# Depthwise convolution: ScalarE opens VectorE's two tap chains in PSUM, three ring slots in place of four, and sums left apart in four chunks

## The reference

```python
def conformer_conv(h, w1, b1, w_dw, b_dw, ln_g, ln_b, w2, b2):
    u = jnp.einsum('bsd,de->bse', h, w1) + b1
    a, gate = jnp.split(u, 2, axis=-1)
    u = a * jax.nn.sigmoid(gate)
    u = lax.conv_general_dilated(
        u, w_dw[:, None, :].astype(u.dtype),
        window_strides=(1,), padding=[(CONV_WIDTH - 1, 0)],
        dimension_numbers=('NWC', 'WIO', 'NWC'),
        feature_group_count=D_MODEL) + b_dw
    u = jax.nn.silu(layernorm(u, ln_g, ln_b))
    return jnp.einsum('bsd,de->bse', u, w2) + b2
```

## Time and profile before

| | us |
|---|---|
| median of 3 runs | 887.62 (887.56 to 887.97) |
| the profiled execution | 887.96 |
| its span, first to last instruction | 886.2 |
| TensorE matmul busy | 875.3 (99%) |
| VectorE busy | 699.4 (79%) |
| ScalarE busy | 463.7 (52%) |
| GpSimd busy | 139.6 (16%) |

### The profile page before, as it was taken

How to read it: one execution, slowest core, us unless ns; L and a number is a source line. 1 busy time by engine, 2 the same in 40 slices (tenths; PEclk the granted TensorE clock), 3 DMA queues, 4 the chain that set the end, 5 groups by cost and what they waited for, 6 DMA issues and landing times.

```text
span 886.2 us, 11890 instructions
## 1 busy us (share of the span) xinstructions
PE 875.3 (99%) x4389; PEld 741.9 (84%) x4389; DVE 699.4 (79%) x941; ACT 463.7 (52%) x672; POOL 139.6 (16%) x122
## 2 busy tenths in 40 slices
PE   8999999999999999999999999999999999999997
PEld 8888897899888888888888889988888888888886
DVE  5799999778886968676878788897786968776866
ACT  5798886247272544536273544637272544536243
POOL 1599970560000020000000040000000000000000
PEclk9999999999999999999999999999999999999999
DMA  9667733305413142331314222122313142331202
GB/s 304 181 162 169 180 62 116 143 1 190 143 48 142 49 170 78 128 124 65 142 48 166 68 78 93 48 94 97 142 47 142 51 175 77 122 129 61 72 1 95
DMA packets 49255, 97.62 MB, mean 110 GB/s; under 512 B 1562, under 2 KB 18978, under 8 KB 48324
## 3 DMA queue, kind: packets, MB, share of 16 engines
q1 hardware_dynamic: 48068, 89.54, 29.1%
q0 software_dynamic: 1008, 7.34, 4.0%
q10 hardware_dynamic: 144, 0.26, 0.1%
HBM read 87.70 MB, written 2.10 MB: 101 GB/s over the span
## 4 chain that ended last, share of the span: by engine, by line
PE 83%; DVE 14%; ACT 1%; issue 1%; POOL 0%; DVEq 0%; POOLq 0%; ACTq 0%
PE ps L1415 16%; PE ps L1413 16%; PE ps L1414 16%; PE ps L1668 10%; PE ps L1666 10%; PE ps L1667 10%; DVE ps L969 8%; PE ps L1432 2%; PE ps L1448 1%; PE ps L1580 1%; PE ps L1585 1%; PE ps L1581 1%; DVE ps L964 1%; DVE tok L878 1%; DVE relu L969 1%
## 5 line engine op out<-in xcount | busy, mean ns | idle before, releaser
L1413 PE MATMUL ps<-act_hi,w_hi 128*128 128x512 f32 (+1 forms) x688 | 254.9, 370 | 0.0
L1414 PE MATMUL ps<-act_lo,w_hi 128*128 128x512 f32 (+1 forms) x688 | 254.2, 369 | 0.0
L1415 PE MATMUL ps<-act_hi,w_lo 128*128 128x512 f32 (+1 forms) x688 | 254.2, 369 | 0.0
L1666 PE MATMUL ps<-w_hi,u_hi 128*128 128x512 f32 x392 | 152.7, 390 | 0.0
L1668 PE MATMUL ps<-w_hi,u_lo 128*128 128x512 f32 x392 | 152.7, 390 | 0.0
L1667 PE MATMUL ps<-w_lo,u_hi 128*128 128x512 f32 x392 | 152.5, 389 | 0.0
L675 ACT ACTIVATE relu<-ps 128x512 f32<-128x512 f32 x36 | 21.5, 597 | 242.8 <-PE ps L1415 242.8
L1413 PEld LDWEIGHTS ps<-act_hi,w_hi 128*128 128x128 f32 x688 | 129.7, 188 | 21.8
L1415 PEld LDWEIGHTS ps<-act_hi,w_lo 128*128 128x128 f32 x688 | 129.6, 188 | 21.8
L1414 PEld LDWEIGHTS ps<-act_lo,w_hi 128*128 128x128 f32 x688 | 129.7, 188 | 21.7
L1150 DVE TENSOR_TENSOR w_lo<-w_raw,w_hi 128x1024 fp32r<-128x1024 f32 x70 | 85.1, 1221 | 58.0 <-ACT w_hi L696 58.0
(11 more groups left out here) (233 smaller groups left out, 1267.6 us busy)
## 6 DMA issues: line engine op xcount, KB each, us to landing
w_raw<-in_mlp_w SPq DMA_DIRECT2D x32, 1024.0 KB, 4.9
w_raw<-in_mlp_w SPq DMA_DIRECT2D x16, 2048.0 KB, 7.9
w_raw<-in_conv_w SPq DMA_DIRECT2D x16, 512.0 KB, 5.4
prod_a<-prod_a POOLq DMA_DIRECT2D x7, 1024.0 KB, 8.3
w_raw<-in_conv_w SPq DMA_DIRECT2D x2, 2048.0 KB, 11.5
h<-in_x SPq DMA_DIRECT2D x4, 512.0 KB, 5.6
out<-tok SPq DMA_DIRECT2D x7, 256.0 KB, 2.0
gain<-in_norm_mlp SPq DMA_DIRECT2D x2, 512.0 KB
```

Of the source, the lines that this page charges most:

```text
L1413: nc.tensor.matmul(dst, lh, rh, start=(n == 0), stop=False)
L1414: nc.tensor.matmul(dst, lh, rl, start=False, stop=False)
L1415: return nc.tensor.matmul(dst, ll, rh, start=False, stop=(n == count - 1))
L1666: nc.tensor.matmul(dst, lh, rh, start=(f == 0 and (opens or i not in (0, 5))), stop=False)
```

## The change

Sharing out (`SHARE`, `POOLED`, `BEGUN`): the slots take six taps rather than eight, three slots wide (`WIDE`) rather than four. The two taps behind them are multiplied by ScalarE too (`BEGUN`), not into `prod_a` but into the two PSUM banks from which the gate and the value half have just been read, the first together with the bias (`begin`, the activation in `products`); they stand ahead of ScalarE's other products and behind `glu_ok`. VectorE's two opening steps are accumulations that take these banks as their addend, and wait for `begin_ok`. In chunk 6 GpSimd adds up seven taps and VectorE has 16 rather than 17.

The join no longer stands at the end of a chunk but behind the gate product of the next one. In chunks 0, 2, 4 and 6 (`APART`) there is none: the last step of the second chain writes into a free slot of `prod_a` (`second_chain`), a memset of one column sets `conv_ok`, and TensorE turns both. TensorE waits for `begun_ok` ahead of the products that overwrite the two banks. The taps of chunk 7 are shared as before.

```diff
-POOL_SHARE = 6
-SHARE = (8, 8, 8, 8, 8, 8, 8, 12)
-WIDE = 4
+POOLED = (6, 6, 6, 6, 6, 6, 7, 0)
+SHARE = (6, 6, 6, 6, 6, 6, 6, 12)
+APART = (0, 2, 4, 6)
+WIDE = 3
+BEGUN = 2
...
+        def begin(e, n):
+            return ps[:, 2 * (e % 2) + 1 - n, :]
+
+        second_chain = prod_a[:, 3 * WIDE + 2, :]
...
             def products(e):
 
                 act.wait_ge(glu_ok, e + 1)
+                for n in range(BEGUN):
+                    t = POOLED[e] + SHARE[e] + n
+                    nc.scalar.activation(begin(e, n), upad[:, e % 2, t:t + S], ACT.Identity, scale=params[:, e, t:t + 1],
+                                         bias=0.0 if n else params[:, e, TAPS:TAPS + 1]).then_inc(begin_ok, 1)
                 pool_products(e, range(3))
...
+            def join(e):
+
+                nc.vector.tensor_tensor(relu[:, e % 2, :], relu[:, e % 2, :], ps[:, 7, :], ALU.add).then_inc(conv_ok, 1)
...
+                if e:
+                    dve.wait_ge(dve_self, self_at[0])
+                    if e - 1 in APART:
+                        nc.vector.memset(stats[:, 4, 36:37], 0.0).then_inc(conv_ok, 1)
+                    else:
+                        join(e - 1)
                 dve.wait_ge(glu_ok, e + 1)
...
+                    if e in APART and n % 2 and n + 2 >= len(own):
+                        into = second_chain
+                        if e >= 2:
+                            dve.wait_ge(conv_turned, e - 1)
+                    if n < 2 and not end:
+                        dve.wait_ge(begin_ok, BEGUN * e + n + 1)
+                        nc.vector.scalar_tensor_tensor(into, window, weight, begin(e, n), ALU.mult,
+                                                       ALU.add).then_inc(begun_ok, 1)
+                        continue
...
-                dve.wait_ge(dve_self, self_at[0])
                 if end:
+                    dve.wait_ge(dve_self, self_at[0])
                     nc.vector.memset(stats[:, 4, 37:38], 0.0).then_inc(conv_ok, 1)
-                else:
-                    nc.vector.tensor_tensor(relu[:, s, :], relu[:, s, :], sums[1], ALU.add).then_inc(conv_ok, 1)
...
                 pe.wait_ge(conv_ok, e + 1)
+                if e in APART:
+                    turn_into(e, second_chain)
```

More of the change, by code:

```diff
@@ L34 @@
 POOL_RING = 6
-POOL_SHARE = 6
-SHARE = (8, 8, 8, 8, 8, 8, 8, 12)
-WIDE = 4
+POOLED = (6, 6, 6, 6, 6, 6, 7, 0)
[3 more added lines that the diff above has]
+BEGUN = 2
 POOL_LAST = 6
 FIRST = tuple(sum(SHARE[:e]) for e in range(NC + 1))
+POOL_FIRST = tuple(sum(POOLED[:e]) for e in range(NC))
+POOL_ADDS = tuple(sum(POOLED[:e]) - e for e in range(NC))
 WINDOWS = (2, 4, 8, 16)
@@ L187, in hybrid_encoder @@
         fold_one = [sem(f"fold_one{k}") for k in range(2)]
+        begin_ok, begun_ok = sem("begin_ok"), sem("begun_ok")
         conv_ok, conv_turned, ctok_ok = (sem(n) for n in ("conv_ok", "conv_turned", "ctok_ok"))
@@ L229, in hybrid_encoder @@
         prod_d = tok[:].rearrange("p a (k t) -> p (a k) t", t=S)
-        LAST_SLOT = (4, 5, 6, 7, 8, 9, 10, 11)
+        LAST_SLOT = (3, 4, 5, 9, 6, 7, 8, 10)
         def slot(e, n):
@@ L252, in hybrid_encoder, with pool_read, begun_taps @@
         merged = (merged_a[:], merged_b[:])
-        def pooled_taps(e):
-            return POOL_SHARE if e < NC - 1 else 0
+        def pool_read(k):
+            e = max(i for i in range(NC - 1) if POOL_FIRST[i] <= k)
+            return POOL_ADDS[e] + max(k - POOL_FIRST[e], 1)
+        def begun_taps(e):
+            return BEGUN if e < NC - 1 else 0
         def piece(k):
@@ L411, in _ @@
                 into = merged[e % 2]
-                for t in range(1, POOL_SHARE):
+                for t in range(1, POOLED[e]):
                     if t == 3:
@@ L425, in _ @@
             pool.wait_ge(glu_ok, NC)
-            pool.wait_ge(padd_ok, (POOL_SHARE - 1) * (NC - 1))
+            pool.wait_ge(padd_ok, POOL_ADDS[NC - 1])
             for n in range(POOL_LAST):
@@ L541, in pool_products @@
                 for t in which:
-                    k = POOL_SHARE * e + t
+                    k = POOL_FIRST[e] + t
                     if k >= POOL_RING:
-                        old = k - POOL_RING
-                        act.wait_ge(padd_ok, (POOL_SHARE - 1) * (old // POOL_SHARE) + max(old % POOL_SHARE, 1))
+                        act.wait_ge(padd_ok, pool_read(k - POOL_RING))
                     nc.scalar.activation(pool_ring(k), upad[:, e % 2, t:t + S], ACT.Copy,
@@ L559, in products @@
                         act.wait_ge(fold_one[(e - 1) % 2], folds(e - 1))
-                    product_of(e, n, POOL_SHARE + n)
-                pool_products(e, range(3, POOL_SHARE))
+                    product_of(e, n, POOLED[e] + n)
+                pool_products(e, range(3, POOLED[e]))
             def last_products(which):
@@ L949, in conv_chunk @@
                 end = e == NC - 1
-                own = range((POOL_LAST if end else pooled_taps(e)) + SHARE[e], TAPS)
+                own = range((POOL_LAST if end else POOLED[e]) + SHARE[e] + begun_taps(e), TAPS)
                 for n, t in enumerate(own):
                     window, weight = upad[:, s, t:t + S], params[:, e, t:t + 1]
-                    if n >= 2:
+                    if n == 1 and e:
+                        dve.wait_ge(conv_ok, e)
+                    elif n in (2, 3) and not end:
+                        dve.wait_ge(begun_ok, BEGUN * e + n - 1)
+                    elif n >= 2:
                         dve.wait_ge(dve_self, self_at[0] - 1)
@@ L1477, in glu_product @@
                     pe.wait_ge(glu_ok, e - 1)
+                    pe.wait_ge(begun_ok, BEGUN * (e - 1))
                 for a in range(2):
@@ L1493, in product_turn @@
                 pe.wait_ge(glu_ok, e)
+                pe.wait_ge(begun_ok, BEGUN * e)
                 for n in which:
@@ L1506, in conv_turn @@
                         pe.wait_ge(ctok_ok, e - 1)
-                    pe.wait_ge(padd_ok, (POOL_SHARE - 1) * (e + 1))
+                    pe.wait_ge(padd_ok, POOL_ADDS[e + 1])
                     turn_into(e, merged[e % 2], first=True)
```

4 lines of the change are left out of this document (2 added, 2 removed).

## The result

| | before | changed |
|---|---|---|
| median of 22 runs, us | 887.66 | 889.57 |
| ratio | | 1.0018 (1.0012 to 1.0024) |
| the profiled execution, us | 887.96 | 889.91 |
| its span, us | 886.2 | 888.2 |

The account below looks back on a forecast made before the run. VectorE's chain and TensorE's products both bind at chunk 7. Chunk 0 +0.91, chunks 1 to 5 +0.70, chunk 6 12.23 for 12.76 give +1.07 us: 889.03 profiled, 888.7 as median; range 886.9 to 889.9.

Parts of the forecast that it names:

- h: ScalarE's pass into PSUM plus hand-over to VectorE, ahead of a chunk's first tap: forecast 0.92 us, bounds 0.62 to 1.03.
- step 3: VectorE's first tap waits 0.78 us plus h behind G; the second product and the deferred join cost nothing.
- Rival B: Faster: h below 0.77 us at each first tap, freed joins outweigh the wait, down to 886.75 us; chance 0.15.
- The sum of the waits: VectorE, gate product to gate product: chunk 0 +0.91 us, chunks 1 to 5 +0.14 each, chunk 6 12.23; chunk 7 +1.07.
- the factor of 7: The shift of chunk 7's gate product was put at 7h - 5.37 us, never below -0.87.
- step 4: Chunk 0: ScalarE's cast stands ahead of its products, so VectorE's first tap starts only at 31.91 us plus h.
- step 1: TensorE's turns in chunks 1, 3, 5 lose 0.44 us each; chunk 7's sigmoid could start at 118.03, gain at most 0.87.
- the floor: Chunk 7's sigmoid waits for TensorE's products, so a faster VectorE alone would gain nothing there.
- the last one of the sum: End of the convolution: TensorE's end shifts by about 0.9 us, VectorE stays last, the rest moves as a whole.
- G: Start of VectorE's gate product (L945) in a chunk; chunk 7's was forecast at 120.70 us against 119.63.
- D: GpSimd or the ring becomes the bound in chunk 6, its sum over 2 us late at TensorE: 889.7 us; chance 0.05.
- C: Slower by more: PSUM write or hand-over costs more, h from 1.02 us on, 889.4 us and up; chance 0.13.

Follow-up runs that it names:

- e10_mixed: Changed kernel without opening products in chunk 0, GpSimd seven taps there, bias moved to GpSimd's first product: 887.42 us, ratio 0.9995.
- e6_later: Changed kernel with 50 filler transposes and one of GpSimd's products put ahead of ScalarE's two opening ones: 892.52 us, ratio 1.0058.
- e2_apart6: Changed kernel with sums left apart in chunk 6 alone, joins back in chunks 0, 2 and 4: 889.76 us, ratio 1.0023.
- e5_first: Changed kernel with 9 filler transposes and chunk 0's two opening products ahead of ScalarE's cast: 888.27 us, ratio 1.0006.
- e9_joins: Kernel before with only the joins moved behind the next gate product: 888.20 us, ratio 1.0001.
- e1_fill: Changed kernel with 16 unread identity transposes in TensorE's wait ahead of the first turn of chunk 7: 888.35 us, ratio 1.0006.
- e12_mixed_again: The kernel of e10_mixed measured once more beside other runs of the kernel before: 887.43 us, ratio 0.9996.

## Why the prediction was right and wrong

*The size of h (step 3): right.* Forecast 0.92, measured 0.89; the passes were put at 0.80 and 0.71 and took 0.79 and 0.67. The 0.09 that the forecast added for the bias pointer is what it costs: the first pass of a pair takes 0.786 with it and 0.693 without (e10_mixed). The Trainium skill (ScalarE: Activation LUTs, step-by-step section) says that ScalarE writes faster to PSUM than to SBUF. By that rule, the trace agrees: the multiplication takes 0.67 or 0.68 into PSUM and 0.71 into `prod_a`, and with a bias pointer as well, 0.786 into PSUM and 0.804 into `prod_b` (e10_mixed). The difference is 0.02 to 0.04. Rival B needed 0.15 to come from h = 0.92 down to 0.77, and 0.3 for its 0.62.

*The sum of the waits: right.* The period was put at 12.89 and is 12.86 or 12.87; chunk 0 at 13.67 and is 13.66; chunk 6 at 12.23 and is 12.21. The gate product of chunk 7 was put 1.07 later and is 0.91 later; the difference is 0.01 in chunk 0, some 0.025 in each of five chunks and 0.02 in chunk 6, and e6_later confirms the factor of 7. The joins do hide in the wait (the 0.91 and 0.33 above, and e2_apart6), and the order of things in chunk 0 is what step 4 said, as e5_first shows by removing it.

*TensorE (step 1): right as arithmetic.* The sigmoid of chunk 7 was put at 118.0 and started at 118.24, untied from TensorE as forecast. In e9_joins the floor binds at chunk 6, and TensorE's pace leaves no room under 89.28 at chunk 7.

*The step that failed* is the last one of the sum: "ScalarE's products for chunk 7 shift with G, TensorE's end by about 0.9, so VectorE stays last, and the rest of the program moves as a whole". It let TensorE keep its pace across a wait. Step 1 had TensorE done sooner with its earlier turns, the sum had the products of chunk 7 later, and the two sentences together make the idle 1.93 us that the text never formed. Behind it the granted clock fell to 0.50 for some three microseconds in the profiled execution, and by times and mean clocks in 13 of 22 runs. With the clock at 1.00, first turn to last takes 11.07 (e1_fill) rather than 12.29; from 122.00 that would have put the last turn at 133.07, and its result 1.08 later at 134.15, just where VectorE stood ready (135.37 - 1.18 = 134.19). So VectorE and TensorE come out even when the clock holds, and 1.2 us late when it does not. The median of the changed kernel fell into the upper group because that group holds 13 of 22.

*The rivals.* D had TensorE delayed by GpSimd's sum; TensorE was indeed what delayed the end, but not by that: in the changed kernel the row of `merged_a` follows without idle time. B and C fell with h.

*What was lucky.* The number came near because two misses of opposite sign met. Without the clock's fall it would have been too high: the nine lower runs have a median of 888.21, and e1_fill lies 0.46 over its kernel before. The fall, which the sum does not have, then put 13 of 22 runs into a group whose own median, 890.04, lies outside the range.

*Where the small differences come from.* In e1_fill the distance from the first gate product to the statistics is 0.90 longer than before, and the time only 0.46, with an interval of -0.3 to +1.3 us. The rest of the program does not give the difference back: from the statistics to the end of the span lie 752.8 or 752.9 us in all fourteen profiles (886.2 - 133.38 before, 888.2 - 135.37 in the changed kernel, 886.3 - 133.50 in e1_fill). So it does move as a whole, as the prediction said. What differs is the stretch ahead of the convolution: the first gate product starts at 30.35 in the profile before and at 29.57 in that of e1_fill, and between 29.57 and 30.55 in the others. Whether kernels made from the changed one come to it earlier on average stays open; it starts at 29.57 to 30.17 in nine profiles of them, and at 29.71 to 30.55 in five made from the kernel before.

## What to carry to other kernels

When a change takes work from one engine and moves the start of another's later, subtract the two and ask whether an engine that was never idle now is; on TensorE such a gap of two microseconds made the turns behind it 1.2 us longer here, in the execution in which the clock is seen to fall, and 16 unread transposes in it bought that back. A hand-over that costs 0.1 us more than what it frees is paid once per chunk, so the passes that stand between two engines should be the shortest there are (one pointer rather than two, nothing ahead of them). An operation moved ahead in one engine's order is a delay for whoever waits on what it passed (e5_first), so follow that engine to the end of the stretch too.

## What the runs showed of the hardware

- ScalarE, 128x512 fp32 with the scale as a pointer: 672 to 693 ns into PSUM (changed kernel and e10_mixed), 712 on average into SBUF. With a bias pointer as well: 786 into PSUM, 804 into SBUF (e10_mixed).
- VectorE took up ScalarE's result 0.10 behind the pass's end (0.89 - 0.79), ScalarE VectorE's 0.03 (44.60 against 43.83 + 0.74).
- TensorE's granted clock behind one idle time, by profile and by the groups of the times, kernel by kernel: 1.93 us of idle time, fallen in 13 of 22 runs; 3.25 us, in 10 of 10; 3.32 us, in 3 of 5; 1.40 us, in 2 of 11; 1.60 us, in none of 11; 0.65 us, in none of 5; 0.43 us or less, in none of 44 (e1_fill, e10_mixed, e12_mixed_again, e5_first). The idle time is that of the profiled execution (for 3.32 and 1.40 us one of those in which the clock did not fall); the other runs of a kernel need not have the same. Why the clock falls in some runs and not in others stays open, and no run here was made to tell that.
